# Branch products of the 512 sample tokens in one group instead of two, and the order of the tasks that follow them

## The reference

```python
ga, gb, gc = jnp.split(jax.nn.sigmoid(pg), N_BRANCH, axis=-1)
merged = ga * (ya @ wb[0]) + gb * (yb @ wb[1]) + gc * (yc @ wb[2])
return merged @ lp['w_out'], S_a, S_c
...
x = x + g1 * mix
h = rms_norm(x, lp['norm2']) * (1 + sc2) + sh2
...
q = (hb @ lp['p_wq']).reshape(P_BLOCK, P_HEADS, 2, P_KEY_DIM // 2)
s1 = jnp.einsum('thd,nd->thn', q[:, :, 0], lp['p_key1'])
...
act = jax.nn.gelu(jnp.einsum('td,thkd->thk', hb, u_tab[expert]))
return jnp.einsum('thk,thkd->td', gate * act, v_tab[expert])
```

## Time and profile before

| what | us |
|---|---|
| median of 3 runs | 3255.39 |
| range | 3243.78 to 3260.89 |
| the profiled execution, device time | 3254.83 |
| its span in the trace | 3252.7 |
| VectorE busy | 1864.4 (57%) |
| TensorE busy | 2756.4 (85%) |
| expert gathers (queue q0) | 671.13 MB, 50.1% of the 16 engines' span |
| other transfers (queue q1) | 142.92 MB, 12.6% |

### The profile page before, as it was taken

The page is one execution under the profiler, slowest core; times in us unless marked ns, Lnnn a source line. Parts: engine busy times, 40 slices in busy tenths (PEclk is TensorE's granted clock), DMA queues, the critical chain, the costliest instruction groups (busy, mean ns, idle before and its releaser), DMA issues.

```text
span 3252.7 us, 45370 instructions
## 1 busy us (share of the span) xinstructions
PE 2756.4 (85%) x16290; PEld 1650.2 (51%) x16290; DVE 1864.4 (57%) x3972; ACT 899.7 (28%) x2374; POOL 888.8 (27%) x812
## 2 busy tenths in 40 slices
PE   7989998898999999887888778898977777777776
PEld 5746665676666666666454334454532233222322
DVE  1029977544333333335787687786477666765454
ACT  2013332014222212122223233333223322332233
POOL 0000000000000000001443444444455555555553
PEclk9999997999999999889999899999999999999999
DMA  5113220211111111055999999999999999999997
GB/s 218 51 39 109 100 87 15 97 52 49 34 33 34 34 33 34 17 211 222 414 419 401 417 407 414 412 419 397 391 420 420 421 408 420 418 417 420 420 420 299
DMA packets 148450, 816.57 MB, mean 251 GB/s; under 512 B 16328, under 2 KB 33480, under 8 KB 62889
## 3 DMA queue, kind: packets, MB, share of 16 engines
q0 software_dynamic: 92160, 671.13, 50.1%
q1 hardware_dynamic: 56104, 142.92, 12.6%
HBM read 800.10 MB, written 13.89 MB: 250 GB/s over the span
## 4 chain that ended last, share of the span: by engine, by line
DMA 27%; PE 12%; issue 5%; DVE 4%; POOL 2%; ACT 2%; POOLq 0%; ACTq 0%; DVEq 0%; PEldq 0%
DMA pr_rows<-in_p_uv,pr_now 27%; PE pr_psy L2621 9%; DVE pr_rows L2964 3%; POOL pr_rows L2496 2%; PE pr_pss L2579 2%; ACT pr_diag L2728 1%; ACT pr_weight L2709 1%; ACT pr_act L2721 0%; DVE pr_acc L2976 0%; PE pr_pss L2552 0%; PE pr_pss L2562 0%; PE pr_pss L2599 0%; PE pr_psy L2541 0%; DVE pr_top_i L2881 0%; ACT pr_s L2698 0%
## 5 line engine op out<-in xcount | busy, mean ns | idle before, releaser
L2621 PE MATMUL pr_psy<-pr_rows,pr_diag 128*128 128x512 f32 x2432 | 1155.1, 621 | 348.1 <-ACT pr_diag L2728 304.5
L2496 POOL DMA_INDIRECT pr_rows<-in_p_uv,pr_now x640 | 793.1, 1239 | 863.5 <-PE pr_psy L2621 759.7
L2621 PEld LDWEIGHTS pr_psy<-pr_rows,pr_diag 128*128 128x128 f32 x2432 | 455.9, 196 | 1010.9 <-issue 655.9
L2964 DVE CUSTOM_DVE_ANT_0 pr_rows<-pr_rows,h_tok 128x1024 f32<-128x1024 f32 x376 | 458.5, 1225 | 319.4 <-DMA pr_rows<-in_p_uv,pr_now 316.0
L2964 DVE CUSTOM_DVE_ANT_0 pr_rows<-pr_rows,pr_h_tok 128x1024 f32<-128x1024 f32 x256 | 311.8, 1226 | 155.2 <-DMA pr_rows<-in_p_uv,pr_now 151.9
L1806 POOL TENSOR_TENSOR yT<-rw_sys,rw_bmask 128x128 f32<-128x128 f32 x40 | 18.1, 453 | 1298.9 <-DVE rw_sys L1905 1298.9
L2721 ACT ACTIVATE pr_act<-pr_dot 128x2 f32<-128x2 f32 x316 | 64.2, 203 | 1111.1 <-DVEq L2970 1110.9
L1310 PE MATMUL rw_gate_ps<-hT,rw_gate_w 128*128 128x320 f32 x768 | 269.4, 473 | 2.8 <-ACT rw_gate L1299 2.8
L2728 ACT ACTIVATE pr_diag<-con,pr_weight 128x128 f32<-128x128 f32 x632 | 216.3, 389 | 0.2
L1310 PEld LDWEIGHTS rw_gate_ps<-hT,rw_gate_w 128*128 128x128 f32 x768 | 133.3, 194 | 58.0 <-issue 16.0
L2709 ACT ACTIVATE pr_weight<-pr_gate,pr_act 128x1 f32<-128x1 f32 (+1 forms) x640 | 153.8, 287 | 22.9
(11 more groups left out here) (442 smaller groups left out, 3464.1 us busy)
## 6 DMA issues: line engine op xcount, KB each, us to landing
hg_ada_w<-in_w_ada SPq DMA_DIRECT2D x16, 1024.0 KB, 5.4
rw_gate_w<-in_w_in SPq DMA_DIRECT2D x24, 512.0 KB, 4.1
early<-in_w_branch SPq DMA_DIRECT2D x24, 512.0 KB, 11.3
pr_rows<-in_p_uv,pr_now POOLq DMA_INDIRECT x640, 12.6
st_ada_w<-in_w_ada SPq DMA_DIRECT2D x4, 2048.0 KB, 24.9
hg_w<-in_w_in SPq DMA_DIRECT2D x16, 512.0 KB, 3.6
early<-in_w_out SPq DMA_DIRECT2D x16, 512.0 KB, 8.0
early<-in_p_wq SPq DMA_DIRECT2D x16, 512.0 KB, 8.0
```

The source lines that it names most:

```text
L2496: nc.gpsimd.indirect_dma_start(out=rows[:, r].rearrange("p u d -> p (u d)"), out_offset=None, in_=A["p_uv"], in_offset=bass.IndirectOffset ...
L2621: last = nc.tensor.matmul(ps_y[:, c % 2, a], diag[:, r], rows[:, r, 1, a * 512:(a + 1) * 512], start=(first and r == 0), stop=False, skip_ ...
L2964: nc.vector.tensor_tensor_reduce(out=rows[:, r, 0], in0=rows[:, r, 0], in1=h_tok[c % 2], scale=1.0, scalar=0.0, op0=ALU.mult, op1=ALU.add, ...
```

## The change

- The 24 branch tasks now each cover all 512 sample tokens (`LP:T`), once. Groups remain for `out`, `sums` and `q`. Eight of the branch tasks stay ahead of the first turn; the other 16 lie in halves 0 to 9 of chunk 0.
- A gate tile is 512 tokens wide. The ring keeps its size in bytes and has 4 tiles instead of 8 (`GRING`).
- `part` is 512 wide and shares its memory with the token buffer `h_tok1`, which is written later.
- The order of all later tasks is new, as the table shows. Routing part 4, the first of chunk 1, is done in 8 steps instead of 12.

```diff
-                            sp.dma_start(K.early_gate[:, o], A["gate_scratch"][o, :, LP:LP + GW].rearrange(
-                                "g p t -> p g t")).then_inc(rest_in, 16)
+                            sp.dma_start(K.early_gate[:, m - 5], A["gate_scratch"][m - 5][:, LP:T]).then_inc(rest_in, 16)
...
-GROUPS, GW, GRING = 2, 2 * P, 8
+GW, GRING = 2 * P, 4
...
-        part = sb("part", [P, 2, GW])
+        part = sb("part", [P, 2, LS])
...
-        plan("branch", EARLY, ((0, 0), [2] * 8))
-        plan("out", 0, ((0, 9), [2, 1] * 2 + [2]))
-        plan("sums", 0, ((0, 15), [1]))
-        plan("q", 0, ((0, 18), [2] * 4))
-        plan("tok", 1, ((0, 22), [1]))
-        plan("scores", 1, ((0, 23), [1]))
+        plan("branch", EARLY, ((0, 0), [2, 1, 2, 2, 1, 2, 2, 1, 2, 1]))
+        plan("out", 0, ((0, 11), [2, 1, 2, 1, 2]))
+        plan("sums", 0, ((0, 17), [1]))
+        plan("q", 0, ((0, 20), [2, 1, 2, 1, 2]))
+        plan("tok", 1, ((0, 24), [1]))
+        plan("scores", 1, ((0, 25), [1]))
+        plan("out", KD, ((0, 27), [1] * KD))
         plan("tok", 2, ((1, 4), [1]))
-        plan("branch", BRANCHES, ((1, 0), [1, 2] * 6))
+        plan("sums", 1, ((1, 4), [1]))
+        plan("q", KD, ((1, 7), [1] * 5))
         plan("scores", 2, ((1, 12), [1]))
-        plan("branch", BRANCHES + 18, ((1, 14), [2, 1] * 2))
-        plan("out", KD, ((1, 19), [1] * KD))
-        plan("sums", 1, ((1, 28), [1]))
-        plan("q", KD, ((1, 31), [2, 2, 1, 2, 1]))
+        plan("q", KD + 5, ((1, 14), [1] * 3))
...
                 def gate(i):
-                    g, m = divmod(i, BRANCHES)
                     sp.wait_ge(br_taken, i - GRING + 1)
-                    sp.dma_start(mg[:, i % GRING], A["gate_scratch"][m][:, tokens(g)]).then_inc(g_in[i % GRING], 16)
+                    sp.dma_start(mg[:, i % GRING], A["gate_scratch"][i][:, LP:T]).then_inc(g_in[i % GRING], 16)
...
+                for n in range(RINGW, len(LOADED)):
+                    weights(n)
+                    if 2 * n - GRING < BRANCHES:
+                        gate(2 * n - GRING)
+                        gate(2 * n - GRING + 1)
...
-                ROUTING = {0: [(1, 0, 4), (2, 4, 20), (3, 20, 36), (4, 50, 62)],
+                ROUTING = {0: [(1, 0, 4), (2, 4, 20), (3, 20, 36), (4, 54, 62)],
```

More of the change, by code:

```diff
@@ L2338, in peer_stage @@
         y_tok = sb("y_tok", [P, D])
-        h_tok1 = sb("h_tok1", [P, D])
+        h_tok1 = part[:].rearrange("p a t -> p (a t)")
         rstd = sb("rstd", [P, GW])
@@ L2342, in peer_stage @@
         sq = q_s
-        h_tok = [h_tok0[:], h_tok1[:]]
+        h_tok = [h_tok0[:], h_tok1]
         ps_s = ctx.enter_context(nc.psum_tensor("pr_pss", [P, 2, HEADS_P, NKEYS], F32))
@@ L2409, in peer_stage @@
             task for at in sorted(TASKS) for task in TASKS[at] if task[0] != "tok"] + [("scores", 4)]
+        USES = [task for task in USERS if task[0] in ("branch", "out", "q")]
+        LOADED = [task for task in USES if task[0] != "branch" or task[1] % 2 == 0]
+        load_of = lambda what, i: LOADED.index((what, i - i % 2 if what == "branch" else i))
         since = lambda n: n - max(m for m in range(n) if USERS[m][0] == "scores") - 1
@@ L2427, in tile @@
         def tile(what, i):
-            return tiles[:, BANK[what, i], 0:GW]
+            return tiles[:, BANK[what, i], 0:LS if what == "branch" else GW]
         def tokens(g):
@@ L2439, in weights @@
                 def weights(n):
[L2440 to L2451 removed]
+                    what, i = LOADED[n - RINGW]
@@ new lines, in weights @@
+                    if what == "branch":
+                        sp.wait_ge(br_mm, i + 2)
+                    elif what == "out":
+                        sp.wait_ge(out_mm, i + 1)
+                    else:
+                        sp.wait_ge(q_mm, i + 1)
+                    what, i = LOADED[n]
+                    if what == "branch":
+                        ins = sp.dma_start(wpair(n), A["w_branch"][i:i + 2].rearrange("a p k n -> p a k n"))
+                    elif what == "out":
+                        ins = sp.dma_start(w[:, n % RINGW], A["w_out"][i % KD])
@@ L2461, in _ @@
-                for g in range(GROUPS):
-                    for m in range(LOADS):
-                        if LOADS * g + m >= RINGW:
-                            weights(LOADS * g + m)
-                        if RINGW <= m < PAIRS:
-                            gate(BRANCHES * g + 2 * m)
-                            gate(BRANCHES * g + 2 * m + 1)
-                        elif g == 0 and m >= LOADS - RINGW:
-                            gate(BRANCHES + 2 * (m - LOADS + RINGW))
-                            gate(BRANCHES + 2 * (m - LOADS + RINGW) + 1)
+                    sp.dma_start(mg[:, i % GRING], A["gate_scratch"][i][:, LP:T]).then_inc(g_in[i % GRING], 16)
@@ L2545, in task @@
                     if what == "branch":
-                        g, j = divmod(i, BRANCHES)
-                        m, b = MERGE_ORDER[j]
-                        n = LOADS * g + j // 2
+                        m, b = MERGE_ORDER[i]
+                        n = load_of(what, i)
                         weights(n)
@@ L2551, in task @@
                         for k in range(KW):
-                            last = nc.tensor.matmul(tile(what, i), wpair(n)[:, j % 2, k], K.yT[b][:, k, tokens(g)],
+                            last = nc.tensor.matmul(tile(what, i), wpair(n)[:, i % 2, k], K.yT[b][:, k, LP:T],
                                                     start=(k == 0), stop=(k == KW - 1))
@@ L2555, in task @@
                     elif what == "out":
-                        g, x = divmod(i, KD)
-                        n = LOADS * g + PAIRS + x
-                        pe.wait_ge(summed, BRANCHES * (g + 1))
+                        g, n = i // KD, load_of(what, i)
+                        pe.wait_ge(summed, BRANCHES)
                         weights(n)
@@ L2572, in task @@
                     elif what == "q":
-                        g, x = divmod(i, KD)
-                        n = LOADS * g + PAIRS + KD + x
+                        g, n = i // KD, load_of(what, i)
                         pe.wait_ge(shifted, KD * (g + 1))
@@ L2802, in between @@
                             softmax(next_part(0, i))
-                        if i == 12:
+                        if i == 13:
                             take_tok(1)
@@ L3027, in branch @@
                 def branch(i):
-                    g, j = divmod(i, BRANCHES)
-                    m, b = MERGE_ORDER[j]
+                    m, b = MERGE_ORDER[i]
                     dve.wait_ge(br_mm, i + 1)
                     dve.wait_ge(gated, i + 1)
-                    dst = hs_[:, m, own(g)] if b == 0 else part[:, b - 1]
+                    dst = hs_[:, m] if b == 0 else part[:, b - 1]
                     nc.vector.scalar_tensor_tensor(out=dst, in0=mg[:, i % GRING], scalar=1.0, in1=tile("branch", i),
@@ L3038, in branch @@
                         dve.wait_ge(summed, i)
-                        nc.vector.tensor_tensor(hs_[:, m, own(g)], hs_[:, m, own(g)], dst, ALU.add).then_inc(summed, 1)
+                        nc.vector.tensor_tensor(hs_[:, m], hs_[:, m], dst, ALU.add).then_inc(summed, 1)
                     else:
```

19 lines of the change are left out of this document (3 added, 16 removed).

## The result

The changed kernel takes 3242.26 us (median of 20 runs, 3221.35 to 3249.07), beside 3261.27 us of the kernel before (20 runs). The ratio is 0.9939, with a 95% interval of 0.9927 to 0.9952: faster by 0.6%, or 19.0 us. Forecast were 3240 us, and 15 us less than before.

A forecast was written before the change was run, and what follows sets the result against it. The stage was taken as bound by what the 16 DMA engines must carry, plus few places where compute frees ring slots too late. 3254.8 - 15.5 - 1 - 6 + 2.5 + 5 = 3239.8, forecast 3240 us, range 3230 to 3253.

The forecast's parts named there:

- Term 1: Branch weights fetched twice: 12 loads of 512 KB vanish from chunk 1, 6.29 MB, a gain of 15.5 us.
- Term 2: Gate loads: same bytes, but 20 loads of 256 KB instead of 40 of 128 KB, a gain of 1 us.
- Term 3: Group 1's queries at the start of chunk 2: single instead of two a half turn, relieving TensorE, a gain of 6 us.
- Term 4: Stage's start: eight wider branch tasks and later gates delay the first dot product to about 1541.5 us, a loss of 2.5 us.
- The cover: At the stage's start: a DMA backlog of 12.1 MB lasts till 1552 us, hiding GpSimd's next gather at 1550 us.
- Term 5: Turn from chunk 0 to 1: routing part 4 in 8 steps tightens VectorE, a loss of 3 us there and 2 after.
- Edits at nothing: Branch tasks in the turns, later gate requests, `part` sharing memory with `h_tok1`, and moved sums and tokens: counted as no cost.
- The signs: Observations named beforehand: five that would show the prediction right, three, on ScalarE's waits, DMA share and VectorE, wrong.
- Everything hidden: Rival: stage start and chunk turn cost nothing and the queries' change gives all, 3231 us; chance 0.2.
- VectorE as the bound: Rival: VectorE bounds 1870 to 2050 us and the start loses its full 11 us, 3252 us; chance 0.2, VectorE or start.
- Late gates: Rival: in-turn gates land late and ScalarE stands, 3304 us; decides against the change from 18.6 us of landing; chance 0.05.
- The rule that was weighed: DMA queues: whether engines alternate by single pieces or whole packets of 9 to 17 descriptors; equal counts were read as single pieces.

The follow-up runs named there:

- e2: Changed kernel plus twelve unused 512 KB loads of branch weights, ahead of twelve of the second group's weight loads: median 3259.27 us, ratio to before 1.0006.
- e11: Changed kernel with each gate fetched in the turns as two loads of 256 tokens instead of one of 512: stage 1721.2 us against 1714.8.
- e3: Changed kernel with the second group's w_out products, sums and queries put back where they were before: stage 6.6 us longer, ratio to before 0.9968.
- e13: Kernel before with the second group's queries spread 1, 1, 2, 1, 1, 2 over half turns instead of 2, 2, 1, 2, 1: stage 1728.0 us against 1732.0 and 1727.9.
- e1: Changed kernel with four branch tasks ahead of the first turn instead of eight: stage 1708.2 us against 1714.8, ratio to before 0.9935.
- e4: Changed kernel with a ring of six wide gate tiles instead of four: stage 1707.8 us against 1714.8, ratio to before 0.9947.
- e7: Changed kernel with branch weights laid out so a pair loads as one 4 KB run per partition, not two of 2 KB: stage 1713.7 us, ratio to before 0.9958.
- e12: Kernel before with only routing part 4 changed, to 8 steps instead of 12: stage 1733.7 us against 1732.0 and 1727.9.
- e8: Changed kernel with a ring of six gates and six branch tasks ahead of the first turn: stage 1706.9 us against 1714.8, ratio to before 0.9926.
- e9: Changed kernel with six gates, six branch tasks ahead of the first turn and paired weights: median 3233.8 us, stage 1704.8 us, ratio to before 0.9917.

## Why the prediction was right, and which of its terms were not

The way it went is the one that was forecast, and so is what made it. But the forecast is better than its parts. The time lies 2 us beside it because two errors of base and size offset each other: the 20 runs of the kernel before have a median 6 us above the three that the forecast started from, and the gain is 19.0 us (16 to 24), not 15. Within the gain, several terms were mis-sized, and they cancel.

**The bound** was named rightly. VectorE still waits for rows, and 12 loads put back take the whole gain away (e2).

**Term 1**, 15.5 us: right, 14.9 by e2.

**Term 2**, 1 us: open as time. In the packet records of the kernel before, from 1560 to 1700 us, a piece of 1 KB holds an engine for 47 ns on average and one of 2 KB for 85 ns. 5120 of the first instead of 2560 of the second, over 16 engines, would make 1.4 us, an estimate from these records. e11 shows that the landing of the gates matters more than that.

**Term 3**, 6 us: too high as a gain at that place. Chunk 2 is 7.1 us shorter, but 1.0 MB fewer bytes fall into it, which is 2.5 us; 4.5 are engines that are better filled (6.8 to 7.1 us lost before, 2.2 to 2.7 now, in the table below). Of e3's 6.6 us only some 2 belong here. The step "two of them make 14.6 us" is not borne out: e13 took one of three pairs away and gained nothing. And the 2.1 us that the prediction leaves for the turn to chunk 3 were read at the wrong place: 2650 to 2670 us lies 50 us and more behind ScalarE's row of chunk 2 (2599.23), and from 2560 to 2640 us the core moves 418 to 421 GB/s, so that this turn costs nothing. How the 4.5 us divide, between TensorE's load and the work at the turn, was not taken apart.

**Term 4**, 2.5 us: this one was mis-sized. The stretch of 20 to 100 us after the first gather lost 8.6 us where the kernel before lost 1.2, so it is 7.4, and e1 and e4 get 7 to 8 back. Its mechanism held, as the changed kernel's start shows (start us, us, engine line op, idle before):

```profile
1518.76 27.73 PE L2544 MATMUL pr_pss<-yT,early 128*128 128x512 f32 x64 [1.97 <-ACT pr_s L2688]
...
1528.64 1.14 POOL L2489 DMA_INDIRECT pr_rows<-in_p_uv,pr_now  x1 [0.28 <-POOL pr_now L2482]
...
1546.78 0.63 ACT L2756 ACTIVATE early<-early 128x512 f32<-128x512 f32 x1 [13.60 <-DMA early<-gate_scratch]
...
1549.93 0.63 ACT L2756 ACTIVATE early<-early 128x512 f32<-128x512 f32 x1 [2.53 <-DMA early<-gate_scratch]
...
1552.02 1.22 DVE L2954 CUSTOM_DVE_ANT_0 pr_rows<-pr_rows,h_tok 128x1024 f32<-128x1024 f32 x1
...
1560.81 1.95 POOL L2489 DMA_INDIRECT pr_rows<-in_p_uv,pr_now  x1 [22.13 <-PE pr_psy L2611]
```

Gate eight was put at 17 us after the first gather (1537.5), and it was opened 21.3 us after it, at 1549.93, 3.4 us after the last product (1518.76 + 27.73 = 1546.49); gate seven was opened at 1546.78. So the gates held the start and not TensorE; ScalarE's wait for gates up to 1700 us was

```profile
ACT early L2756 <- DMA early<-gate_scratch: 34.8, 6, 13.6
```

The first dot product came 23.4 us after the first gather, where the forecast's 1541.5 is 20.8. GpSimd's next gather came 32.2 us after its first, where the forecast had 29. The cover was worked out as 12.1 MB lasting till 1552, 31.3 us after the first gather, and "the cover just holds" compared this with the issue, 29. That step failed. A backlog that ends near the issue of the next gather is a hole, and behind it the rows fit slots that come free one after the other, at the pace of compute: the four 20 us stretches from 20 us after the first gather on moved 316, 372, 397 and 414 GB/s, with VectorE busy for 17.7 to 18.2 us of each. By e7 (first dot at 21.2 us, 5.3 us more lost than before) the forecast's own 20.8 us would have cost some 5 us; the gates' 2.6 us added the rest.

**Term 5**, 5 us: too high by about as much. GpSimd waited for part 4

```profile
POOL pr_now L2482 <- DVE pr_experts L2920: 7.4, 1, 7.4
```

which is in the 6 to 10 us named, but the turn cost 1.5 us of DMA, less than the 2.1 of before, and 5 more were forecast. In the kernel before the same routing in 8 steps does cost some 3 us (e12). In the changed kernel w_out loads for group 1 lie beside it, so that the DMA has other work to do while the gathers are late; without them it lost 3.4 us more there (e3). The prediction's own 22.1 against 22.7 us a turn said that this just fits, and I charged 3 + 2 us for it nevertheless.

**Edits at nothing.** One was worth something. Where VectorE scales `hs_` after the sums of group 0, the kernel before falls to 357 GB/s for 20 us (1740 us; 349 in its second trace), a loss of 3.0 to 3.4 us. In the changed kernel the same work comes 33 us later, counted from the first gather, and the lowest stretch behind it (1788.64 to 1808.64 us) has 397 GB/s, 1.1 us. Why it costs less there was not looked for.

**The sum.** The stage's gain splits into bytes and into time in which the engines were not full. For each chunk, its bytes, and its time less these bytes at 420 GB/s, the level of the quiet stretches (first and second trace of each kernel):

| chunk | before, MB | before, not full, us | after, MB | after, not full, us |
|---|---|---|---|---|
| 0 | 158.0 | 10.1, 9.3 | 162.5 | 14.2, 15.9 |
| 1 | 148.5 | 6.1, 4.6 | 139.7 | 3.6, 3.1 |
| 2 | 136.7 | 7.1, 6.8 | 135.7 | 2.7, 2.2 |
| 3 | 135.2 | 3.4, 3.3 | 134.4 | 4.9, 4.2 |
| 4 | 127.6 | 9.7, 9.7 | 127.5 | 10.1, 10.0 |
| all | 705.9 | 36.4, 33.8 | 699.7 | 35.4, 35.5 |

6.2 MB less are 14.8 us, and the time that is lost is the same in both kernels, within the 2.6 us by which the two traces of the kernel before differ. So the second pass's bytes are the whole gain; what the start loses, chunks 1 and 2 and the work after the sums give back. The prediction had the same balance, -1 - 6 + 2.5 + 5 = +0.5 us, out of terms of which two were wrong by some 5 us each (term 4 too low, term 5 too high): that part is luck. The medians of the runs differ by 19.0 us, the stages by 15.1, and the interval of the ratio allows 16 to 24. What of the remaining 1 to 9 us is real stays open; the mixer part's spread hides it.

**The signs.** Of those named for right, four came: q1 at 136.63 MB, chunk 1 shorter by 22.8 us, 411 GB/s in 2250 to 2350 us, GpSimd's wait at 7.4 us. The fifth did not: the first dot product came at 1552.02 us, and the hole was 8.6 us and not under 3. And two of the signs for wrong came, both at the start: a DMA share of 0.81 in 1560 to 1580 us, and ScalarE waiting for gates in the turns, if only 5.5 and 2.0 us.

**The rivals.** *Everything hidden* (3231, or 24 us less than before) was wrong for the changed kernel, but e8 and e9 reach it: 26 and 27 us below the median of the kernel before. *VectorE as the bound* did not come: in 1870 to 2030 us it was busy for 15.2 to 19.2 of 20 us, and the core moved 415 to 421 GB/s but for the one stretch of 387 at the turn. *Late gates*: gates landed after 10.7 us in the median of 1550 to 1650 us, far from 18.6.

**The rule that was weighed.** By the Trainium skill (DMA: Bandwidth & Descriptors, Queues, rings and completion order) an engine drains a whole packet, typically some 9 to 17 descriptors, before it turns to another queue. The equal counts of the earlier trace rows were weak evidence against it: in that stretch a half turn asks for 4 x 128 pieces of gathers and for 256 of a weight load and 2 x 128 of gates, so the counts are equal however the engines take turns. Shorter stretches of the kernel before are better. The two queues (packets, MB, share of the 16 engines; a packet of the profile is one piece, or the 4 bytes of a semaphore) while nothing but a load of branch weights (2 KB pieces) was landing, 1557 to 1560 us, and while one of w_out (4 KB pieces) was, 1624 to 1627 us:

```profile
q0 software_dynamic: 136, 0.99, 80.2%
q1 hardware_dynamic: 139, 0.26, 22.4%
```

```profile
q0 software_dynamic: 111, 0.79, 63.4%
q1 hardware_dynamic: 112, 0.46, 37.6%
```

If loads are spread evenly, an engine has 8 pieces of a gather and of a w_out load, and 16 of a branch weight load. Whole loads in turn would make the first pair of counts one to two, and a w_out load would wait behind up to 8 pieces of a gather, which take 0.32 us each. It is one to one, and the w_out load has 17 packets started in its first half microsecond (1623.78 to 1624.28 us), beside 20 of the gathers' queue. So the trace doesn't agree with turns of 9 to 17 pieces; it looks like turns of a single one.
